# Making and storing the last hidden tile of a Strassen MLP two to three units later

## The reference, cut to what matters

```
hid = jax.nn.relu(jnp.einsum('btd,df->btf', rms_norm(x, norm2_g[l]), w_up[l]))
x = x + jnp.einsum('btf,fd->btd', hid * hid, w_down[l])
```

## Time and profile before

| | us |
|---|---|
| median of three runs | 2369.08 |
| profiled execution, its own time | 2368.17 |
| its span from first to last instruction | 2366.5 |
| PE (matmul) busy in the span | 2309.7 |
| DVE busy | 1644.6 |
| ACT busy | 1122.3 |
| mean granted TensorE clock, share of full | 0.991 |

### The profile page before, as it was taken

How to read it: one execution, slowest core, us unless ns; L and a number is a source line. 1 busy time by engine, 2 the same in 40 slices (tenths; PEclk the granted TensorE clock), 3 DMA queues, 4 the chain that set the end, 5 groups by cost and what they waited for, 6 DMA issues and landing times.

```text
span 2366.5 us, 44046 instructions
## 1 busy us (share of the span) xinstructions
PE 2309.7 (98%) x17246; PEld 2137.8 (90%) x17246; DVE 1644.6 (69%) x2198; ACT 1122.3 (47%) x1735; POOL 391.4 (17%) x658
## 2 busy tenths in 40 slices
PE   8999999999999999699999999999999999999999
PEld 7999999955555669699999999999899999999999
DVE  6355455444454466898888888888777888887887
ACT  6244445633332353356555555556544444444443
POOL 0071000154555510000000000000311111110200
PEclk9999999999999999899999999999999999999999
DMA  6332232599999976045555555554995757564643
GB/s 195 108 96 97 78 102 90 205 349 379 363 380 357 375 280 234 38 132 206 198 189 196 181 199 202 192 194 168 363 282 189 226 166 234 170 215 156 241 141 119
DMA packets 147808, 490.24 MB, mean 207 GB/s; under 512 B 28905, under 2 KB 32618, under 8 KB 136466
## 3 DMA queue, kind: packets, MB, share of 16 engines
q1 hardware_dynamic: 92418, 250.70, 31.5%
q0 software_dynamic: 55184, 236.73, 27.5%
HBM read 408.43 MB, written 78.91 MB: 206 GB/s over the span
## 4 chain that ended last, share of the span: by engine, by line
PE 94%; DVE 4%; issue 1%; ACT 1%; DMA 1%; SPq 0%; ACTq 0%; DVEq 0%
PE bank L2616 19%; PE bank L2619 19%; PE bank L2612 19%; PE bank L580 15%; PE bank L585 7%; PE bank L2503 4%; PE bank L2478 3%; PE bank L2438 2%; PE bank L2380 1%; PE bank L2280 1%; PE bank L2409 1%; PE bank L2486 1%; PE bank L2394 1%; DVE x_res L2113 0%; PE bank L2383 0%
## 5 line engine op out<-in xcount | busy, mean ns | idle before, releaser
L580 PE MATMUL bank<-x_act,w_hi 128*128 128x364 f32 (+1 forms) x1728 | 377.5, 329 | 0.1
L2612 PE MATMUL bank<-hid_in,down_ring 128*128 128x272 f32 x1792 | 280.2, 288 | 5.9 <-issue 4.0
L2612 PE MATMUL bank<-x_op,ring 128*128 128x272 f32 x1792 | 263.1, 289 | 18.5 <-ACT x_op L1188 12.0
L2616 PE MATMUL bank<-hid_in,down_ring 128*128 128x272 f32 x1792 | 280.2, 289 | 0.0
L2619 PE MATMUL bank<-hid_in,down_ring 128*128 128x272 f32 x1792 | 280.1, 288 | 0.0
L580 PEld LDWEIGHTS bank<-x_act,w_hi 128*128 128x128 f32 x1728 | 275.4, 188 | 1.6 <-DVE w_lo L1604 1.0
L2616 PE MATMUL bank<-x_op,ring 128*128 128x272 f32 x1792 | 263.8, 289 | 2.3 <-DVE x_op L2124 2.3
L2619 PE MATMUL bank<-x_op,ring 128*128 128x272 f32 x1792 | 262.0, 288 | 0.0
L2612 PEld LDWEIGHTS bank<-x_op,ring 128*128 128x128 f32 x1792 | 240.1, 189 | 19.8 <-issue 19.8
L1188 ACT ACTIVATE lines<-bank 128x272 f32<-128x272 f32 x240 | 95.5, 398 | 338.0 <-PE bank L2619 337.9
L2612 PEld LDWEIGHTS bank<-hid_in,down_ring 128*128 128x128 f32 x1792 | 246.8, 189 | 6.3 <-issue 4.2
(11 more groups left out here) (302 smaller groups left out, 3593.6 us busy)
## 6 DMA issues: line engine op xcount, KB each, us to landing
up_raw<-w_up SPq DMA_DIRECT2D x128, 512.0 KB, 4.2
hid_parts<-hid_out POOLq DMA_DIRECT2D x32, 1904.0 KB, 6.5
w_raw<-weights SPq DMA_DIRECT2D x43, 1024.0 KB, 4.9
hid_in<-hid_parts POOLq DMA_DIRECT2D x71, 544.0 KB, 5.3
down_raw<-w_down SPq DMA_DIRECT2D x96, 384.0 KB, 4.2
v_ring<-sb_v POOLq DMA_DIRECT2D x128, 256.0 KB, 5.2
v_ring<-fox_v POOLq DMA_DIRECT2D x120, 256.0 KB, 4.9
hid_in<-hid_parts POOLq DMA_DIRECT2D x96, 272.0 KB, 3.9
```

The lines of the kernel that those rows point to most:

```text
L580: ins = nc.tensor.matmul(bank[:, base + b, 0:n], hi, row[:, t:t + n], start=begin, stop=end)
L2612: mm(out, part_of(n, 0)[:, cols], operand(k)[:, 0], start=(first and k == 0), stop=False, skip_group_check=True)
L2616: mm(out, part_of(n, 0)[:, P * k:P * k + P], operand(k)[:, 1], start=False, stop=False, skip_group_check=True)
```

## The change

The relu, the squares, the mixes and the split of hidden tile 31 move from the steps around unit 32 to units 33, 34 and 35. The store of tile 31 on POOL now stands behind the five loads of tile 4 instead of ahead of them. The instructions themselves, their sizes and their number stay.

```diff
--- before.py
+++ after.py
@@ -1169,9 +1169,10 @@
             load_first(o)
         load_hidden(FIRST_TILES, 2)
         load_hidden(FIRST_TILES + 1)
+        load_hidden(FIRST_TILES + 2)
         store_hidden(LAST)
         added_rows = 0
-        for i in range(FIRST_TILES + 2, HID_LOADS):
+        for i in range(FIRST_TILES + 3, HID_LOADS):
             while added_rows < ROW_PAIRS and i >= HID_SLOTS and added_rows < user_of(i - HID_SLOTS):
                 add_rows(added_rows)
                 added_rows += 1
@@ -1576,13 +1577,21 @@
                 op_high_part(n + RING)
             if n in X_HIGH_AT:
                 x_high(X_HIGH_AT[n])
-            if o == P4 and v < UP_UNITS:
+            if o == P4 and v < UP_UNITS - 1:
                 first_relu(v)
-            if o == P3 and v < UP_UNITS:
+            if o == P3 and v < UP_UNITS - 1:
                 first_squares(v)
                 second_squares(v)
-            if o == P6 and 1 <= v <= UP_UNITS:
+            if o == P6 and 1 <= v < UP_UNITS:
                 hidden_high(v - 1)
+            if (v, o) == (UP_UNITS + 1, P6):
+                first_relu(UP_UNITS - 1)
+            if (v, o) == (UP_UNITS + 1, P5):
+                first_squares(UP_UNITS - 1)
+            if (v, o) == (UP_UNITS + 1, P4):
+                second_squares(UP_UNITS - 1)
+            if (v, o) == (UP_UNITS + 2, P5):
+                hidden_high(UP_UNITS - 1)
 
 
     @block.vector
@@ -2215,11 +2224,15 @@
                 op_low_part(n + RING)
             if o == P1:
                 sum_4(u)
-            if o == P2 and 1 <= u <= UP_UNITS:
+            if o == P2 and 1 <= u < UP_UNITS:
                 mix_hidden(u - 1)
+            if (u, o) == (UP_UNITS + 2, P2):
+                mix_hidden(UP_UNITS - 1)
+            if (u, o) == (UP_UNITS + 3, P2):
+                hidden_low(UP_UNITS - 1)
             if o == P2 and u > UP_UNITS + ROW_PAIRS:
                 join_b(u - 1)
-            if o == P5 and 1 <= u <= UP_UNITS:
+            if o == P5 and 1 <= u < UP_UNITS:
                 hidden_low(u - 1)
             if o == P4 and u >= UP_UNITS + ROW_PAIRS:
                 join_a(u)
```

## The result

The changed kernel took 2376.83 us (median of 6 runs, 2374.65 to 2380.24), the kernel before 2368.93 (6 runs, 2366.69 to 2371.01). The ratio is 1.0037, 95% interval 1.0027 to 1.0048: slower by about 8 us, clear of noise. The profiled execution of the changed kernel was its fastest, 2374.65 us with a span of 2372.9.

The account below looks back on a forecast made before the run. PE, working 2309.7 of 2366.5 us, bounds the kernel, so only its idling or slowing counts. 2368.2 - 0.6 (units 32, 33) + 8.9 (unit 37's wait and half clock) = 2376.5, median 2377; 8-in-10 range 2366 to 2383.

Parts of the forecast that it names:

- PE's 3.97 us wait at P6 goes: Unit 32: with the squares moved away, ACT copies P1's bank at once, so PE's 3.97 us wait disappears.
- unit 33 can't begin before 1690.1: Unit 33's P1 needs tile 2, landed at 1690.1, so PE's idle time only moves and this brings 0 us.
- 0.6 for weights asked for earlier: Unit 34's weights, asked for some 4 us earlier, run against tile 2's loads: 0.6 us cost, between 0 and 1.3.
- Rival 3: Unit 33: tile 2's landing didn't gate PE; with q0 keeping pace, all 10.0 us come back: 2359, chance 0.08.
- Net of both parts: 0.6 us gained.: Units 32 and 33: 1.2 us gained by clearing DVE's work, less 0.6 for earlier weights; between -0.5 and 3.7.
- the set charge for half clock: Slow matmuls after PE idles, in unit 33 and behind unit 37's wait: 2.5 us charged each time.
- "I take 0" for the moved work: Units 34 and 35: slack of 3.2 us covers the moved high part (1.79 us) and low part (2.13): 0 us.
- The store at 1719.8, tile 6 at 1741.6, PE idle 6.4.: Late store holds up tiles 5 and 6, so PE idles 6.4 us in P1 of unit 37.
- The sum.: Whole kernel: 2368.2 - 0.6 + 8.9 = 2376.5 us for the profiled execution, 2377 as the median.
- Rival 1: Unit 37: q0 at 392 GB/s lands tile 6 at 1735, no wait worth naming; 2365 to 2369, chance 0.15.
- Rival 2: Unit 37: equal turns give q0 half, 196 GB/s; 14.4 us of waiting plus 2.5 half clock; 2385, chance 0.07.

Follow-up runs that it names:

- store 30 moved: Changed kernel, tiles 5 and 6 loaded before tile 31's store, tile 30's store behind tile 2's loads: 2368.43 us; behind tile 3's, tile 31's work one unit later: 2364.25 us.
- tiles 5 and 6 first: Changed kernel with the loads of tiles 5 and 6 also ahead of the store of tile 31: 2367.74 us, ratio 0.9997 to the kernel before.
- the order alone: Kernel before with only tile 4's loads put ahead of the store of tile 31, ACT and DVE as before: 2371.66 us, ratio 1.0014.
- late store alone: Kernel before with tile 4's loads ahead of tile 31's store, that store held until DVE's low part of unit 35's P4: 2376.98 us, ratio 1.0037.
- the gap: Kernel before with tile 4's loads ahead of tile 31's store, that store held until unit 34's P2 is done: 2368.01 us, ratio 0.9997.

## Why the prediction was right

*"PE's 3.97 us wait at P6 goes" and "unit 33 can't begin before 1690.1".* Right. ACT's copy came at once, and P1 of unit 33 stood until tile 2 had landed. In the frame of unit 32 this was at 12.0 us instead of 11.1; I had allowed 0.6 for weights asked for earlier and it was 0.9. They were asked for 4.2 us earlier counted from unit 32 (at 1679.81; before, at 1685.31), and tile 2 landed at 11.8 to 12.1 us in the three kernels that have the work moved and store 30 as before, at 10.7 to 11.2 in the four that don't move it. The runs with store 30 moved show that the landing is the gate. Rival 3, in which landing did not count, is out; yet the meeting of the two times in the kernel before was chance. There PE came to P1 of unit 33 at 1690.10 without a gap, slowed by the half clock, and its third matmul would not have been due before 1690.35.

*"Net of both parts: 0.6 us gained."* It was 1.7. The term that was off is the half clock: I charged 2.5 us as behind the first wait of before, but PE was at 1.2 GHz only from about 1690 to 1693: the 13 matmuls from 1689.72 on took until 1692.7, 3.0 us instead of 1.6, a loss of 1.4. The other 0.25 us is two matmuls of P1 that ran ahead, on tiles 0 and 1, before the wait. But the gain can't be credited to the change. Two kernels in which ACT and DVE work as before also began unit 34 at 20.67 and 20.92 us, because behind their second wait (2.1 us) the clock stayed full. So the term that was mis-sized is the set charge for half clock. I had one size for every wait, and it came out as 1.4 us in the changed kernel and as nothing behind the waits of 2.08 and 2.12 us.

*"I take 0" for the moved work.* Right: the same work, with tiles 5 and 6 first, leaves no wait of PE on ACT or DVE, and a median 0.7 us under the kernel before, within noise.

*The store at 1719.8, tile 6 at 1741.6, PE idle 6.4.* The store came at 1716.9, which is 39.2 us from unit 32 where my figure was 40.8; 1.7 of this is the shift of PE that I had said moves both. It took 8.6 us where I took 7.1 from a store on an idle queue. The weights' queue had 19.1% of the engines' time over 1716 to 1726, against 4.4% over 1653 to 1661 for the store of the earlier trace rows, and tile 5's loads followed at once on q0; no run tells the two apart. Tile 5 needed 6.9 more and PE resumed for tile 6 7.4 after that, where I had 7.33 each. The errors are small. Counted from matmul start to matmul start, tile 6's matmul is 7.5 us late where I had 6.4; the 21 matmuls from 1739.78 to 1744.30 took 4.5 us instead of 2.6, a loss of 1.9 where I took 2.5. The term is 9.4 against 8.9. Nothing new came later, as said: from unit 39 to the end it is 605.5 us in both.

*The sum.* 2376.5 in the frame of the profiled execution, 2377 as a median; measured 2376.83. That it comes within 0.2 us is luck. In the frame of unit 32 the forecast was +8.3 and the profile shows +7.8, and two errors partly cancel in it, 0.5 too little for the wait and its clock and 1.1 too little for units 32 and 33; the six executions themselves spread over 5.6 us. The profiled one, 2374.65, was the fastest of the six; it had gained 1.3 us before the change is reached.

*The rivals.* Rival 1 (q0 keeps pace) fell with the 6.93 us wait. Rival 2 rested on the rule of the Trainium skill (page "DMA: Bandwidth & Descriptors", the section on queues, rings and completion order) that each engine takes turns between queues with work. Over 1715 to 1742, with the store, two tiles and the first additions of the residual on q0 and the weights on q1, the rows (packets, MB, share) were

```profile
q0 software_dynamic: 1398, 6.65, 73.7%
q1 hardware_dynamic: 1135, 2.64, 26.9%
```

so q0 had 73.7% of the engines' time, somewhat more than the 68.8% of the earlier trace rows, and not half. The rule is not refuted. It speaks of turns packet by packet, and the packets are not far from even, 1398 to 1135. But a packet of q0 moved 4.8 KB in the mean and one of q1 2.3 KB, and took longer. The step from equal turns to half of the time, 196 GB/s, was my error in rival 2, and it would have doubled the wait. The run with the order alone shows the side of it that I had not weighed: with the store in flight, q1 gets its loads later.

*What I had overlooked.* Nothing in the prediction said that tile 4's loads ahead of the store could cost anything while the store stays early. The order alone cost 3.2 us in the median. In the changed kernel this didn't show: the late store left q0 free just then, and the weights asked for from 1700 to 1715 landed in 2.9 to 3.9 us.

## What to carry to other kernels

When work is moved later to unblock an engine, follow the transfer at its end: what counts is not when that transfer is needed but what stands behind it on its queue, and when that is needed. A wait that is taken away may only uncover the landing of a load at the same moment, so read landings, not just releasers, before counting it as a gain. Then order the queue by need: with tiles 5 and 6 ahead of the late store the 8 us lost were regained, and with the work one unit later still and both stores behind the urgent loads it became 0.2% gained. And before a difference of 1 or 2 us in one profile is called a gain, look for it in a kernel without the change: here the clock alone made as much.

## What the runs showed of the hardware

The length of the half clock does not follow the length of the wait: in the kernel before PE lost 1.6 us behind 1.93 us of idleness, and in the changed one 1.4 us behind waits of 1.8, 0.9 and 3.9 us in a row, and 1.9 behind 6.9. Nor does it always come: behind a wait of 1.95 us (late store alone) the clock of 1694 to 1696 was 0.50, behind 2.12 and 2.08 us (order alone, without and with the gap) it was 1.00. The earlier waits of the same unit were 3.5, 3.9 and 4.1 us, and no run separates their part.

The same load on SP's queue q1 took 10.9 us in the kernel before, 13.9 with the store of tile 31 in flight beside it for most of that time, and 6.6 with that store held back. When both queues had work the packet counts were near each other (1398 to 1135, 748 to 674, 790 to 699), while the shares of the engines' time were 73.7 to 26.9, 66.1 to 32.3 and 75.9 to 25.9%; q0's packets were the larger ones each time.
